# GpSimd's pooling mixer: each long addition, product and subtraction as two instructions of half the rows

## What is computed

```python
for gi, win in enumerate(POOL_WINDOWS):          # 2, 4, 8, 16
    xg = grp[..., gi, :]
    outs.append(window_mean(window_mean(xg, win, 1), win, 2) - xg)
y = jnp.stack(outs, axis=-2)
y = jnp.einsum('brwgc,gcd->brwgd', y, w_pool)
return y.reshape(B, R * W, POOL_W) * pool_scale
```

## Time and profile before

| | before |
|---|---|
| median of 3 runs | 1319.59 us (1317.67 to 1320.16) |
| the profiled execution | 1317.26 us, its span 1315.5 us |
| PE busy | 1261.0 us, 96% of the span |
| DVE busy | 1035.2 us, 79% |
| GpSimd busy | 668.4 us, 51% |
| ACT busy | 592.9 us, 45% |
| the mixer on GpSimd | 126.94 to 241.75 us from the span's start |

### The profile page before, as it was taken

One profiled execution on the slowest core, in us unless ns is written; L12 is line 12 of the kernel. 1 busy time (PEld: TensorE's weight loads), 2 busy tenths in 40 slices (PEclk: granted clock), 3 DMA queues, 4 the chain that ended last, 5 costly groups with the idle time before them and its releaser, 6 DMA issues.

```text
span 1315.5 us, 21778 instructions
## 1 busy us (share of the span) xinstructions
PE 1261.0 (96%) x7739; PEld 1156.9 (88%) x7739; DVE 1035.2 (79%) x1506; ACT 592.9 (45%) x1029; POOL 668.4 (51%) x503
## 2 busy tenths in 40 slices
PE   6999999999998899989999999999999999999996
PEld 2589999999987778888999999999999988888885
DVE  6455899894567688879887878787875779888898
ACT  5732224545445734555444444444443455345430
POOL 1001999744343011329888888788877874200011
PEclk9999999999999999999999999999999999999999
DMA  9532332473225532203363535444543679945892
GB/s 359 157 88 84 90 94 67 136 240 81 81 81 192 192 113 97 80 33 106 99 204 129 175 120 196 137 160 141 179 147 133 199 238 366 355 134 188 293 322 108
DMA packets 164851, 210.28 MB, mean 160 GB/s; under 512 B 10567, under 2 KB 102819, under 8 KB 164515
## 3 DMA queue, kind: packets, MB, share of 16 engines
q1 hardware_dynamic: 164286, 204.47, 47.4%
q0 software_dynamic: 288, 4.72, 0.9%
q10 hardware_dynamic: 197, 0.06, 0.0%
HBM read 161.49 MB, written 47.72 MB: 159 GB/s over the span
## 4 chain that ended last, share of the span: by engine, by line
PE 51%; POOL 2%; DVE 1%; issue 1%; ACT 0%; POOLq 0%
PE ps L1609 11%; PE ps L1607 11%; PE ps L1608 11%; PE ps L1640 6%; PE ps L1642 6%; PE ps L1641 6%; POOL tlo L2264 0%; POOL ulo L2264 0%; POOL xlo L2264 0%; POOL dwlo L2264 0%; POOL xwlo L2264 0%; PE ps L1166 0%; POOL wsum L2465 0%; DVE z L3275 0%; DVE z L3274 0%
## 5 line engine op out<-in xcount | busy, mean ns | idle before, releaser
L3089 DVE SCALAR_TENSOR_TENSOR ps<-gs,taps,ps 128x945 f32<-128x945 f32 (+2 forms) x176 | 215.7, 1226 | 10.0 <-ACT ps L2042 4.6
L2407 POOL TENSOR_TENSOR rstd<-mv,neghalf 128x1 f32<-128x1 f32 x27 | 25.1, 928 | 258.2 <-DVE mv L3266 156.9
L1259 PE MATMUL ps<-h1hi,whi 128*128 128x384 f32 x432 | 152.9, 354 | 2.7 <-DVE wlo L2603 2.7
L1259 PE MATMUL ps<-h1lo,whi 128*128 128x384 f32 x432 | 145.2, 336 | 0.0
L1259 PE MATMUL ps<-h1hi,wlo 128*128 128x384 f32 x432 | 145.1, 336 | 0.0
L1640 PE MATMUL ps<-dwhi,uhi 128*128 128x512 f32 x290 | 113.1, 390 | 1.3 <-POOL dwlo L2264 1.3
L1642 PE MATMUL ps<-dwhi,ulo 128*128 128x512 f32 x290 | 112.9, 389 | 0.0
L1641 PE MATMUL ps<-dwlo,uhi 128*128 128x512 f32 x290 | 112.8, 389 | 0.0
L1607 PE MATMUL ps<-thi,xhi 128*128 128x288 f32 x320 | 94.3, 295 | 2.0 <-issue 1.1
L2264 POOL TENSOR_TENSOR wlo<-raw,whi 128x512 fp32r<-128x512 f32 x44 | 61.9, 1408 | 65.4 <-ACT whi L1712 29.7
L1609 PE MATMUL ps<-thi,wlo 128*128 128x288 f32 x320 | 94.4, 295 | 0.0
(11 more groups left out here) (444 smaller groups left out, 3998.8 us busy)
## 6 DMA issues: line engine op xcount, KB each, us to landing
raw<-in_w_up SPq DMA_DIRECT2D x78, 256.0 KB, 4.7
u_rows<-val SPq DMA_DIRECT2D x22, 576.0 KB, 2.9
adaw<-in_w_ada SPq DMA_DIRECT2D x24, 512.0 KB, 4.0
st<-in_w_down SPq DMA_DIRECT2D x22, 512.0 KB, 4.3
t_rows<-st SPq DMA_DIRECT2D x11, 1024.0 KB, 4.6
raw<-in_w_in SPq DMA_DIRECT2D x40, 256.0 KB, 4.4
w_raw<-in_w_down SPq DMA_DIRECT2D x33, 256.0 KB, 5.3
v_raw<-u_rows SPq DMA_DIRECT2D x33, 256.0 KB, 4.8
```

What stands on the lines that cost most here:

```text
L1259: last = mm(ps[:, bank, 0:GN], a[:, n % 2, k * P:(k + 1) * P], b[:, kk, grp(g)], start=(kk == 0 and a is whi and b is h1hi), stop=(kk == K ...
L2407: tt(rstd[:, j % 4, :], mv[:, j % 4, 1:2], neghalf[:, 0, :], ALU.pow).then_inc(rstd_ready, 1)
L3089: step(stt(a3[:, ro, co], g3[:, ri, ci], taps[:, tap:tap + 1], a3[:, ro, co], ALU.mult, ALU.add), 2 + m)
```

## The change

A helper `in_two` issues an elementwise operation as two instructions, each of half of the output's second dimension: of the grid's rows where the operand has rows, of the columns where it is flat (the 15 rows of the first group's first addition go as 7 and 8). Only the second one carries the link. All 32 long additions, products and subtractions of the mixer use it: 5, 7, 9 and 11 in the four groups. The context's short instructions, copies and memsets stay.

```diff
+                def in_two(out, x, y, op):
+                    half = out.shape[1] // 2
+                    tt(out[:, 0:half], x[:, 0:half], y[:, 0:half], op)
+                    return tt(out[:, half:], x[:, half:], y[:, half:], op)
+
                 if steps == 1:
                     link(nc.gpsimd.memset(b[:, 0:nlat + PADC], 0.0))
                     nc.gpsimd.tensor_copy(centre(b)[:, 0:1, :], as_rows(xg[:, 0:GRID_W]))
-                    link(tt(centre(b)[:, 1:, :], as_rows(xg[:, 0:LAT - GRID_W]), as_rows(xg[:, GRID_W:LAT]), ALU.add))
+                    link(in_two(centre(b)[:, 1:, :], as_rows(xg[:, 0:LAT - GRID_W]), as_rows(xg[:, GRID_W:LAT]), ALU.add))
...
-                    link(tt(grid(b, 1, GRID_H - 1), xg[:, 0:LAT - GRID_W], xg[:, GRID_W:LAT], ALU.add))
+                    link(in_two(grid(b, 1, GRID_H - 1), xg[:, 0:LAT - GRID_W], xg[:, GRID_W:LAT], ALU.add))
...
-                            link(tt(grid(b, -ext, n_r), grid(a, -ext - far, n_r), grid(a, far - ext, n_r), ALU.add))
+                            link(in_two(grid(b, -ext, n_r), grid(a, -ext - far, n_r), grid(a, far - ext, n_r), ALU.add))
...
-                            link(tt(centre(b), as_rows(grid(a, -far, GRID_H)), as_rows(grid(a, far, GRID_H)), ALU.add))
+                            link(in_two(centre(b), as_rows(grid(a, -far, GRID_H)), as_rows(grid(a, far, GRID_H)), ALU.add))
...
-                        link(tt(dst[..., at:at + n_c], src[..., at - back:at - back + n_c],
-                                src[..., at + ahead:at + ahead + n_c], ALU.add))
+                        form = in_two if dst is bl else tt
+                        link(form(dst[..., at:at + n_c], src[..., at - back:at - back + n_c],
+                                  src[..., at + ahead:at + ahead + n_c], ALU.add))
...
-                link(tt(mid, res, bc(invt[:, g, 0:GRID_H].unsqueeze(2), [P, GRID_H, GRID_W]), ALU.mult))
-                link(tt(res, mid, bc(invt[:, g, GRID_H:GRID_H + GRID_W].unsqueeze(1), [P, GRID_H, GRID_W]), ALU.mult))
+                link(in_two(mid, res, bc(invt[:, g, 0:GRID_H].unsqueeze(2), [P, GRID_H, GRID_W]), ALU.mult))
+                link(in_two(res, mid, bc(invt[:, g, GRID_H:GRID_H + GRID_W].unsqueeze(1), [P, GRID_H, GRID_W]), ALU.mult))
...
-                link(tt(xl, res, xl, ALU.subtract))
+                link(in_two(xl, res, xl, ALU.subtract))
```

## The result

The changed kernel takes 1328.82 us (median of 8 runs, 1323.34 to 1330.92), the kernel before on the same chip 1319.04 us (8 runs, 1316.93 to 1320.79). The ratio is 1.0085, with a 95% interval of 1.0066 to 1.0104: slower by 11 us (8.7 to 13.7). The two profiled executions lasted 1330.62 and 1317.26 us, 13.4 us apart.

A forecast was written before the change was run, and what follows sets the result against it. PE, busy 96%, was taken to bound. Starts 4.2 + turns 4.0 end the mixer 8.2 us later, polo 7.7 late, less 0.62 slack 7.1; against the 1319.59 median, forecast 1326.7 us, range 1320.5 to 1331.5.

The forecast's parts named there:

- What hangs on the mixer's end: Behind the mixer, polo gates ACT's copy, which releases PE's fifth pool product: slack 1.57 us, product 6.1 us late.
- likeliest case: The sum as worked out, from the mixer's later end: +4.5 to +9.5 us (1324 to 1329), chance 0.62.
- the case in which only starts are paid: Rival: in the mixer, halves keep the port together; starts cost 1.6 to 4.2 us, time +1.0 to +3.6, chance 0.13.
- Turns: In the mixer, DVE comes in between halves; 4.0 us of its port time moves ahead of the mixer's end.
- Starts: In the mixer, 32 extra instruction starts on GpSimd cost 1.6 to 4.2 us; 4.2 was taken.
- The first polo: Behind the mixer, the first low part of the products, alone on the port, ends 7.7 us later, at 250.9.
- PE's relief of 1.8 us: At 207 and 221 us PE no longer waits for DVE; this brings nothing, PE reaches the same closed door earlier.
- The conditioning columns: Behind the fifth pool product on PE, released by ACT's fourth product copy: slack 0.62 us, 7.1 us late.
- the shift stays: From 255 us on, the same picture as before, shifted by 7.1 us; PE has no wait up to 297.
- More turns or dearer starts: Rival in the mixer: dearer handovers or another convolution ahead, polo 11 to 14 us late, +10 to +13, chance 0.12.
- DVE gets ahead and PE gains: Rival: the mixer hardly grows, PE's two stalls vanish, everything 1.8 us sooner, 1317.8 us, chance 0.07.
- the delay is taken back: Rival: in the scan or behind it, loads come no later than before, +0 to +3 us, chance 0.06.

The follow-up runs named there:

- hold7: Kernel before, no split, plus seven memsets of 1424 columns on GpSimd between the mixer's end and the first polo: 1325.38 us, ratio 1.0079.
- POOL_FIRST 25: The change with all 32 splits, and the pool products begun one unit later (25 in place of 24): 1320.4 us, ratio 1.0029 to the kernel before.
- in_four: The change with each of the 32 operations as four instructions in place of two, 96 extra: 1339.13 us, ratio 1.0176 to the kernel before.
- last_group: The change in the fourth group's eleven long operations only, groups 1 to 3 as in the kernel before: 1321.78 us, ratio 1.005.
- first_three: The change in groups 1 to 3 only (21 extra instructions), the fourth as in the kernel before: 1326.05 us, ratio 1.0068.
- the kernel before with POOL_FIRST 25: Kernel before, no split, with the pool products begun one unit later (25 in place of 24): 1317.37 us, ratio 1.0007.
- hold2: Kernel before, no split, plus two memsets of 1424 columns on GpSimd between the mixer's end and the first polo: 1320.64 us, ratio 1.0039.
- three_long_pf25: Only the three longest additions (1280, 1792, 1536 columns) in halves, pool products one unit later: 1318.92 us, ratio 1.0021 to the kernel before.

## Why the prediction was right, and what it missed

**What hangs on the mixer's end: as predicted.** The kernel loses by one chain, from polo by ACT's po to PE's fifth product. hold7 gives the loss by that delay alone, and POOL_FIRST 25 takes some two thirds of it away although the mixer is longer. The slack of 1.57 us was nearly right: polo is 8.9 us late and the product 7.5, and in the five other kernels of the table too the product is 1.4 us less late than polo. By the mechanism the prediction was right; the size of its sum wasn't. It had 7.1 us more and 11.2 were measured, above the 4.5 to 9.5 that its likeliest case allowed. That 1328.82 us lies in the stated range is owed to the range reaching up to 1331.5 for a rival whose reasons aren't borne out below, and so partly to luck.

**The halves don't keep the port together.** That they would was an assumption of mine, and the runs show the opposite. The mixer grew by 9.37 us, more than the 1.6 to 4.2 of the case in which only starts are paid. DVE comes in between unlinked halves (195.15 and 196.13 us above), and its five more instructions stand in the window.

**Turns: 4.0 us predicted, 3.0 found.** I had two multiply-adds and the four instructions of the convolution move ahead. Five instructions did, one multiply-add of 0.55 us on the port and the convolution's four. Of these the one of 1023 columns ended 1.08 us after GpSimd had let go, a short one of 127 columns 0.15 after it: 0.55 + 2 × 1.08 + 2 × 0.15 = 3.01. That turns are bounded by DVE's work is what in_four shows (75 of DVE's instructions in the mixer, as with halves).

**Starts: 4.2 us predicted, about 3.4 found. Lost cover: not in the sum, about 2.4.** The growth less the turns is 9.37 − 3.01 = 6.4 us. Divided by 32 that is 0.20 us, but it isn't the price of a start. The timelines allow a closer account: for each instruction of GpSimd, and each of DVE's subtractions and multiply-adds, the time to its end from the end of the last one before it on either of the two engines, or from its own start if that is later. Added up over the mixer in both kernels, the growth is 3.4 us on the 32 operations that were split, 2.7 on DVE's turns, 0.9 in gaps where neither works, and 2.4 on GpSimd's instructions that were not split (each to some 0.3 us, by which of DVE's instructions are counted in):

| kernel | extra instructions | split operations, us | for each extra one | DVE's turns | not split | gaps |
|---|---|---|---|---|---|---|
| changed | 32 | 3.4 | 0.11 | 2.7 | 2.4 | 0.9 |
| last_group | 11 | 0.9 | 0.08 | 3.7 | 0.1 | 0.2 |
| first_three | 21 | 2.6 | 0.12 | 2.2 | 1.1 | 0.6 |
| in_four | 96 | 12.0 | 0.13 | 3.2 | 4.5 | 2.0 |

So an extra start cost no more than the 0.13 us that I read from instructions of 512 and 2304 columns with the port to themselves. What the sum put at nothing is the column "not split". In the changed kernel 1.9 of the 2.4 us are two memsets of 1.29 us. GpSimd's and DVE's rows in the kernel before show one of them in the third group:

```profile
175.13 1.29 POOL L2321 MEMSET poolA<- 128x1424 f32 x1
...
175.66 0.69 DVE L2603 TENSOR_TENSOR wlo<-raw,whi 128x512 fp32r<-128x512 f32 x1
```

and the changed kernel's show the same memset and the next low part, GpSimd's rows first:

```profile
179.51 1.29 POOL L2326 MEMSET poolA<- 128x1424 f32 x1
...
182.13 1.73 POOL L2304 TENSOR_TENSOR poolA<-poolB 128x512 f32<-128x512 f32 x1
...
181.72 1.00 DVE L2609 TENSOR_TENSOR wlo<-raw,whi 128x512 fp32r<-128x512 f32 x1 [3.67 <-ACT whi L1712]
```

Before, DVE's low part ran inside the memset and took 0.69 us, and neither waited for the other. With shorter waits DVE has run out of work by then (3.67 us of waiting for ACT's whi, up to 181.72). The memset stands alone, and the next low part falls between two halves instead, where the second half takes 1.73 us. I expected DVE without work for up to 25 us of the mixer; it is 36.7. This is the part of the sum that I had wrong. The account was made after the fact, and no run was made to test it.

**The first polo: 7.7 us late predicted, 8.9 found.** The mixer's 9.37 us less the 0.47 that polo, alone on the port, is shorter.

**PE's relief of 1.8 us brings nothing: as predicted.** It shows only as a longer wait, 9.7 us for a product that is 7.5 late. ACT too is ready earlier, hence its 16.4 us of wait for polo where I expected about 13.

**The conditioning columns never became the door.** I had them as the later of two (7.1 us after 6.1). In the changed kernel PE doesn't wait there, since it comes late itself, slowed behind the fifth product.

**The clock: missed.** No term of the sum and no rival had it. I took PE to go on at full speed from the end of its wait. It is also 2.9 us slower behind the wait, at a clock of 0.50 and 0.56 up to 260 us, and 2.4 us in hold7. The sixth product is 10.4 us late, counted from the mixer's start, where I had 7.1: 0.4 of the difference comes with the fifth product (7.5 against 7.1), 2.9 with the clock.

**The way to the end.** I said that the shift stays. In the profiled pair it is 11.0 us at the scan's first chunk (0.7 of it there when the mixer begins), 12.3 at 496 us, 14.7 at 590 and 13.4 from 640 us on. The first step comes near 476 us, where the granted clock is at 0.50 for a short piece that the kernel before hasn't. Behind it, one window each over the same stage shows the second, of the changed kernel, the kernel before and first_three:

```profile
564.00:597.80 33.80, 29.30 (x162) 28.25 (x160) 26.07 (x27) 15.33 (x27) 7.49 (x7) 0.95 0.15 48
```

```profile
551.70:583.10 31.40, 27.76 (x162) 26.71 (x161) 23.72 (x26) 14.50 (x26) 6.66 (x7) 1.00 0.17 52
```

```profile
561.00:594.80 33.80, 27.75 (x162) 26.71 (x160) 26.08 (x27) 16.89 (x27) 9.03 (x7) 1.00 0.15 48
```

The same work takes 33.8 us at 0.95 in the first and 31.4 at 1.00 in the second, but 33.8 at 1.00 in the third. So the clock isn't the only way into the long form. In first_three a low part of GpSimd's takes 3.69 us in place of 1.29, and PE waits 2.8 us for it. In the changed kernel, at the clock of 0.95, it starts 1.6 us later and takes 2.1 us. This stage is so long in seven of the ten profiles, six of them at 0.95, that of the kernel before with POOL_FIRST 25 and that of hold2 among them, and short in those of the kernel before, hold7 and three_long_pf25. It doesn't go with the splits.

Such pieces also bear on what one profile says of the end. The kernel before has two of them in the scan, near 390 and 424 us, and hold7 has none. hold7's shift, counted from the mixer's start, is 10.1 us at the scan's first chunk and 5.7 from 450 us on; that its runs are 1.0079 longer rests on their medians. Whether a shift by some microseconds makes such a piece likelier can't be told from one profile of each kernel. Of the 11.2 us of the ratio, the profiles account for 10.4, up to the sixth product: 9.37 of mixer, less 0.47 for the shorter polo and 1.57 of slack, plus 0.15 on ACT's path and 2.88 for the clock.

**The rivals.** "More turns or dearer starts" was, with near 1331 us, as close to the measured time as my likeliest case, and by the difference (10 to 13 us more) it was closer. Its reasons aren't borne out: DVE's turns were no more than I had, and a start was no dearer. The difference came from the lost cover and the clock. That DVE gets ahead and PE gains is excluded by the ratio. That the delay is taken back doesn't hold for the changed kernel, apart from 1.3 us behind 590 us.

## What to carry to other kernels

Before a long instruction is split so that a neighbour gets the port sooner, ask what stands behind the whole sequence in the splitting engine's order: the relief is worth only what reaches the engine that bounds (here 1.8 us of relief brought nothing), while the extra starts arrive at the sequence's end (here 0.08 to 0.13 us each). Ask too what the two engines have done side by side until now, and whether the neighbour, sooner done, will still have work at that time. Where a new wait of several microseconds falls on PE, add what PE may lose behind it at a lower clock (here 1.7 to 2.9 us behind waits of 5.1 to 9.7 us). A bare delay put in at the one place, as in hold7, tests such a theory more cleanly than any part of the change.

## What the runs showed of the hardware

- Turns at the port were bounded by DVE's work: with 0, 32 and 96 extra boundaries DVE had 70, 75 and 75 instructions in the mixer.
- DVE came in at a boundary without a link too: its subtraction, waiting since 195.15, went next, and the half of 1.49 us at 196.13 let 0.55 us of it pass.
- Inside an instruction DVE did not come in: in three_long_pf25 its subtraction of 206.96 us, begun 0.11 us behind a half of 2.12 us on GpSimd, ended only at 209.52, 0.55 us behind that half's end.
- An extra GpSimd instruction cost 0.08 to 0.13 us by itself in this mixer, in line with the 0.13 us worked out from instructions that had the port to themselves. The mixer grew by 0.23 to 0.43 us for each, with DVE's turns and the lost cover.
- A memset on GpSimd and a DVE subtraction with two inputs ran side by side without a wait: 1.29 us from 175.13 and 0.69 us from 175.66.
- In 33 runs of two kernels that differ by two memsets, a mean granted clock lower by 0.001 went with 1.0 us more.
- After waits of PE of 5.1 to 9.7 us its next stretch of 6.6 us took 1.7 to 2.9 us longer, with the granted clock at 0.50 at first. Behind the one of 22.1 us it took 1.7 us longer, no more than behind the one of 5.1: the longest of these waits did not bring the largest loss.
